# One streaming MoE layer on one core: the down weights of an expert loaded as one transfer of four chunks

## The reference

```
gu = xe @ w_gu[e] + b_gu[e]              # (rows, 1024) @ (1024, 2048)
g, u = gu[:, :D_FF], gu[:, D_FF:]
g = minimum(g, 7); u = clip(u, -7, 7)
h = (u + 1) * (g * sigmoid(1.702 * g))   # (rows, 1024), the inner features
y = h @ w_down[e] + b_down[e]            # (rows, 1024) @ (1024, 1024)
```

## Time and profile before

| | us |
|---|---|
| median of 3 runs | 1076.94 (1076.07 to 1077.82) |
| the profiled execution, its own time | 1075.5 |
| its span, first to last instruction | 1073.6 |
| PE (TensorE matmul) busy | 1029.4 (96%) |
| VectorE busy | 317.7 (30%) |
| ScalarE busy | 95.7 (9%) |
| DMA, mean over the span | 391 GB/s, 420.31 MB moved |

### The profile page before, as it was taken

One profiled execution on the slowest core, in us unless ns is written; L12 is line 12 of the kernel. 1 busy time (PEld: TensorE's weight loads), 2 busy tenths in 40 slices (PEclk: granted clock), 3 DMA queues, 4 the chain that ended last, 5 costly groups with the idle time before them and its releaser, 6 DMA issues.

```text
span 1073.6 us, 11705 instructions
## 1 busy us (share of the span) xinstructions
PE 1029.4 (96%) x5101; PEld 491.1 (46%) x5102; DVE 317.7 (30%) x491; ACT 95.7 (9%) x163; POOL 8.3 (1%) x20
## 2 busy tenths in 40 slices
PE   9999999999999999989898989989898989999997
PEld 7767454444444443435353534434353435334333
DVE  3533121332323232322313231323223132313243
ACT  2222130100000000000001010000000010100001
POOL 1100000000000000000000000000000000000000
PEclk9999999999999999999999999989999999999999
DMA  9950779999999999999999999999999999999996
GB/s 356 312 118 1 258 279 408 427 427 427 426 428 427 429 428 429 429 429 426 429 429 429 429 429 430 428 427 429 428 429 429 429 430 428 427 418 418 422 421 263
DMA packets 58543, 420.31 MB, mean 391 GB/s; under 512 B 23045, under 2 KB 23345, under 8 KB 29969
## 3 DMA queue, kind: packets, MB, share of 16 engines
q1 hardware_dynamic: 55840, 419.32, 94.6%
q0 software_dynamic: 352, 0.55, 0.2%
q10 hardware_dynamic: 2320, 0.03, 0.1%
HBM read 418.29 MB, written 1.58 MB: 391 GB/s over the span
## 4 chain that ended last, share of the span: by engine, by line
PE 68%; DMA 30%; issue 0%; SPq 0%; DVE 0%; ACT 0%; DVEq 0%
PE ps L854 35%; DMA ring<-in_w_gu_dram 28%; PE ps L787 7%; PE ps L870 6%; PE ps L709 5%; PE ps L896 3%; PE ps L727 3%; DMA ring<-in_w_down_dram 2%; PE ps L585 2%; PE ps L856 1%; PE ps L881 1%; PE ps L738 1%; PE ps L900 1%; PE ps L1024 1%; PE ps L611 1%; PE ps L677 0%
## 5 line engine op out<-in xcount | busy, mean ns | idle before, releaser
L854 PE MATMUL ps<-ring,xT 128*64 128x512 f32 x1008 | 457.3, 607 | 31.5 <-DMA ring<-in_w_gu_dram 31.3
L856 PE MATMUL ps<-ring,xT 128*64 128x512 f32 x1024 | 464.7, 607 | 0.0
L854 PEld LDWEIGHTS ps<-ring,xT 128*64 128x64 f32 x1008 | 135.6, 139 | 306.4 <-issue 301.9
L870 PE MATMUL ps<-ring,he 128*64 128x512 f32 x480 | 213.5, 594 | 3.4 <-DMA ring<-in_w_down_dram 2.5
L872 PE MATMUL ps<-ring,he 128*64 128x512 f32 x472 | 210.5, 596 | 0.0
L1613 DVE TENSOR_TENSOR x<-ps,x 128x512 f32<-128x512 f32 (+1 forms) x84 | 54.3, 683 | 297.8 <-PE ps L896 271.8
L856 PEld LDWEIGHTS ps<-ring,xT 128*64 128x64 f32 x1024 | 137.6, 139 | 0.0
L870 PEld LDWEIGHTS ps<-ring,he 128*64 128x64 f32 x480 | 63.1, 137 | 133.6 <-issue 133.6
L787 PEld LDWEIGHTS ps<-oh,hn 128*128 128x128 f32 x720 | 89.5, 196 | 8.3 <-issue 6.0
L787 PE MATMUL ps<-oh,hn 128*128 128x128 f32 x720 | 91.5, 282 | 0.0
L1256 ACT COPY gu_sb<-ps 128x1024 f32<-128x1024 f32 x16 | 16.2, 1012 | 607.4 <-PE ps L856 607.4
(11 more groups left out here) (220 smaller groups left out, 623.4 us busy)
## 6 DMA issues: line engine op xcount, KB each, us to landing
ring<-in_w_gu_dram SPq DMA_DIRECT2D x105, 2048.0 KB, 25.8
ring<-in_w_down_dram SPq DMA_DIRECT2D x53, 2048.0 KB, 27.0
ring<-in_w_gu_dram SPq DMA_DIRECT2D x44, 1024.0 KB, 19.6
ring<-in_w_down_dram SPq DMA_DIRECT2D x19, 1024.0 KB, 27.0
w_chc<-in_w_in_dram SPq DMA_DIRECT2D x1, 4096.0 KB, 20.7
w_qkv<-in_w_in_dram SPq DMA_DIRECT2D x4, 768.0 KB, 9.0
w_b<-in_w_in_dram SPq DMA_DIRECT2D x1, 2048.0 KB, 28.3
w_o<-in_w_out_dram SPq DMA_DIRECT2D x2, 1024.0 KB, 28.2
```

The source lines that it names most:

```text
L854: even = mm(gu_banks(j)[0:CAP, n, :], xT[j % 2][:, k, 0:CAP], first[n], start=(k == 0), stop=(k == KT - 1))
L856: odd = mm(gu_banks(j)[CAP:P, n, :], xT[j % 2][:, k, CAP:P], second[n], start=(k == 0), stop=(k == KT - 1))
L870: even = mm(out[0:CAP, half, :], hid[:, f, 0:CAP], first[2 * a + half], start=(f == 0), stop=(f == FT - 1))
```

## The change

An expert's four down chunks get one layout: partition p holds eight neighbouring features of w_down, 32 KB together (`dn_dram` loses its block index), and a load may take up to four chunks (`DN_RUN`). In `ORDER` all four down chunks of the even expert now come before the four of the odd one, where before they alternated by two. `features` takes every eighth column instead of every fourth, the biases come in two transfers of 32 bytes together instead of four of 16, and the values that TensorE waits for are worked out for each load (`per_pass`), since slots no longer all get the same number of loads. FINE, the tail loaded in the order of use, goes from 36 places to 40. The loads of w_gu stay as they are, in size and order.

```diff
-        dn_dram = w_down.rearrange("l e (m p a) n -> (l e) m p (a n)", a=2 * FPC, p=P)
+        GU_RUN, DN_RUN = 2, DNC
+        dn_dram = w_down.rearrange("l e (p a) n -> (l e) p (a n)", p=P)
...
-            for pair, chunks in ((j, range(GUC)), (j - 1, range(GUC, CH))):
+            for pair, chunks, run in ((j, range(GUC), GU_RUN), (j - 1, range(GUC, CH), DN_RUN)):
                 if 0 <= pair < PAIRS:
                     IN_USE += [(2 * pair + s, c) for c in chunks for s in range(2)]
-                    ORDER += [(2 * pair + s, c + a) for c in chunks[::2] for s in range(2) for a in range(2)]
+                    ORDER += [(2 * pair + s, c + a) for c in chunks[::run] for s in range(2) for a in range(run)]
...
-        EARLY, FINE = 3 * GUC, 4 * GUC + 4
+        EARLY, FINE = 3 * GUC, 5 * GUC
...
         while n < RINGED - 2:
-            e, c = ORDER[n]
-            two = (EARLY <= n < RINGED + 1 - FINE and c % 2 == 0 and ORDER[n + 1] == (e, c + 1)
-                   and slot_of(n) < RING - 1)
-            LOADS.append((n, 1 + two))
-            n += 1 + two
+            (e, c), many = ORDER[n], 1
+            room = min(RING - slot_of(n), RINGED - 2 - n, GU_RUN - c % GU_RUN if c < GUC else CH - c)
+            while n >= EARLY and many < room and ORDER[n + many] == (e, c + many):
+                many += 1
+            LOADS.append((n, many))
+            n += many
...
         def features(part, f):
-            m, a = f // (2 * FPC), f % (2 * FPC)
-            first = part * FF + m * 2 * FPC * P + a
-            return slice(first, first + 2 * FPC * (P - 1) + 1, 2 * FPC)
+            first = part * FF + f
+            return slice(first, first + FT * (P - 1) + 1, FT)
...
-                    for q in range(2 * FF // (4 * P)):
-                        sp.dma_start(b_guT[:, :, 4 * q:4 * q + 4],
-                                     b_gu[0].rearrange("e (q p a) -> q p e a", p=P, a=4)[q]).then_inc(bias_in, 16)
+                    for q in range(2):
+                        sp.dma_start(b_guT[:, :, FT * q:FT * (q + 1)],
+                                     b_gu[0].rearrange("e (q p a) -> q p e a", p=P, a=FT)[q]).then_inc(bias_in, 16)
...
-                pe.wait_ge(told, so_far(j, value, PER_LOOP // RING * 16))
+                pe.wait_ge(told, so_far(j, value, per_pass(e, c)))
...
+            def per_pass(e, c):
+
+                return LANDED[(e + 4, c)][1] - LANDED[(e, c)][1] if e + 4 < NE else 0
```

More of the change, by code:

```diff
@@ L309, in hybrid_layer_kernel @@
         ADDED_LATE = 2 * NT * (PAIRS - 2) - 2 * NT
-        gu_dram = w_gu.rearrange("l e (m p a) f -> (l e) m p (a f)", a=2, p=P)
-        dn_dram = w_down.rearrange("l e (m p a) n -> (l e) m p (a n)", a=2 * FPC, p=P)
+        GU_RUN, DN_RUN = 2, DNC
+        gu_dram = w_gu.rearrange("l e (m p a) f -> (l e) m p (a f)", a=GU_RUN, p=P)
+        dn_dram = w_down.rearrange("l e (p a) n -> (l e) p (a n)", p=P)
         IN_USE, ORDER = [], []
         for j in range(PAIRS + 1):
-            for pair, chunks in ((j, range(GUC)), (j - 1, range(GUC, CH))):
+            for pair, chunks, run in ((j, range(GUC), GU_RUN), (j - 1, range(GUC, CH), DN_RUN)):
                 if 0 <= pair < PAIRS:
                     IN_USE += [(2 * pair + s, c) for c in chunks for s in range(2)]
-                    ORDER += [(2 * pair + s, c + a) for c in chunks[::2] for s in range(2) for a in range(2)]
+                    ORDER += [(2 * pair + s, c + a) for c in chunks[::run] for s in range(2) for a in range(run)]
         ALL = len(IN_USE)
-        EARLY, FINE = 3 * GUC, 4 * GUC + 4
+        EARLY, FINE = 3 * GUC, 5 * GUC
         ORDER[:EARLY] = IN_USE[:EARLY]
@@ L327, in hybrid_layer_kernel @@
         EARLY_AT, LATE_AT, PIECES_AT = (1, CH - 1), (NE - 2, 0), (NE - 4, 0)
+        assert sorted(ORDER) == sorted(IN_USE)
         for at in (EARLY_AT, LATE_AT, PIECES_AT):
@@ L370, in features @@
         def features(part, f):
-            m, a = f // (2 * FPC), f % (2 * FPC)
-            first = part * FF + m * 2 * FPC * P + a
-            return slice(first, first + 2 * FPC * (P - 1) + 1, 2 * FPC)
+            first = part * FF + f
+            return slice(first, first + FT * (P - 1) + 1, FT)
         def tile_features(k):
-            first = k // 2 * 2 * P + k % 2
-            return slice(first, first + 2 * P - 1, 2)
+            first = k // GU_RUN * GU_RUN * P + k % GU_RUN
+            return slice(first, first + GU_RUN * (P - 1) + 1, GU_RUN)
         def most_rows(eng):
@@ L410, in rows_of @@
             def rows_of(e, c, many):
-                src = gu_dram[e, c // 2] if c < GUC else dn_dram[e, (c - GUC) // 2]
-                return src[:, c % 2 * FLAT:(c % 2 + many) * FLAT]
+                src, first = (gu_dram[e, c // GU_RUN], c % GU_RUN) if c < GUC else (dn_dram[e], c - GUC)
+                return src[:, first * FLAT:(first + many) * FLAT]
             def load(e, c, many, slot):
@@ L526, in _ @@
             pool.dma_start(w_rt[:, :, :], w_router.rearrange("l (k p) e -> p (l k) e", p=P)).then_inc(router_in, 16)
-            pool.dma_start(g2[:, :].rearrange("p (m a) -> p m a", a=2),
-                           norm2_g.rearrange("l (m p a) -> p (l m) a", a=2, p=P)).then_inc(router_in, 16)
+            pool.dma_start(g2[:, :].rearrange("p (m a) -> p m a", a=GU_RUN),
+                           norm2_g.rearrange("l (m p a) -> p (l m) a", a=GU_RUN, p=P)).then_inc(router_in, 16)
             pool.dma_start(b_rt[:, :], b_router.to_broadcast([P, NE])).then_inc(router_in, 16)
@@ L911, in chunks_of @@
                     [(2 * j - 2 + s, c) for s in range(2) for c in range(GUC, CH)]
+            def per_pass(e, c):
+                return LANDED[(e + 4, c)][1] - LANDED[(e, c)][1] if e + 4 < NE else 0
             for j in IN_LOOP[2:]:
                 for (e, c) in chunks_of(j):
-                    told, value = LANDED[(e - 4, c)]
+                    first = e - (j - IN_LOOP[0]) // 2 * 4
                     assert ORDER.index((e, c)) == ORDER.index((e - 4, c)) + PER_LOOP
-                    assert LANDED[(e, c)] == (told, value + PER_LOOP // RING * 16)
-            ARRIVALS = sorted({LANDED[at][1] for j in IN_LOOP[:2] for at in chunks_of(j)})
+                    assert LANDED[(e, c)][0] is LANDED[(first, c)][0]
+                    assert per_pass(e - 4, c) == per_pass(first, c) > 0
+            ARRIVALS = sorted({(LANDED[at][1], per_pass(*at)) for j in IN_LOOP[:2] for at in chunks_of(j)})
             GROWING = ([(value, 2) for value in range(1, 6)] + [(value, 2 * 2 * NT) for value in range(2, 2 * 2 * NT + 1, 2)]
-                       + [(value, PER_LOOP // RING * 16) for value in ARRIVALS])
+                       + ARRIVALS)
             growing = {}
@@ L1632, in _ @@
                 if j == 1:
-                    dve.wait_ge(bias_in, 4 * 16)
+                    dve.wait_ge(bias_in, 2 * 16)
                     gate_and_up(1, gu_banks(0), 0)
```

## The result

| kernel | median us | against before, 95% interval | its span |
|---|---|---|---|
| before | 1076.94 (5 runs) | | 1073.6 |
| with the change | 1081.60 (5 runs) | 1.0045 (1.003 to 1.0059) | 1078.7 |

The change makes the kernel 0.45% slower: 4.7 us. The forecast was +5.4 us, 1082.3.

A forecast was written before the change was run, and what follows sets the result against it. The prediction took DMA to bound the middle and a TensorE chain hanging on one landing the end. Wait +9.8, given back -4.0, clock +1.7 and rate -2.1 made +5.4 us: 1082.3 us, range 1078.3 to 1088.

The forecast's parts named there:

- The bound and the mechanism: DMA bounds the middle; the last 128 us are a TensorE chain hanging on one landing, so late waits decide.
- The new wait, +9.8: Pair 12's first down matmul must wait for all eight down chunks, beginning at 927.6 instead of 917.80: +9.8 us.
- The rate, -2.1: In the load stream, 26 four-chunk loads before pair 12's down each save a fixed 0.08 us: -2.1 us.
- The 2 us for each DMA: Skill's fixed cost per DMA: 24 loads fewer would give an estimated 48 us if uncovered; the queue was said to cover it.
- What is given back, -4.0: After pair 12's wait, later idle times of 0.29, 2.13, 1.32 and 0.3 us swallow part of the lateness: -4.0 us.
- The transposes, 0: Reading every eighth column in the transposes after pair 12's wait: taken as 0, bounded by 3.4 us either way.
- The clock, +1.7: After pair 12's longer wait TensorE runs a stretch at half clock that nothing absorbs: +1.7 us, ends 0 and 2.9.
- The sum: Whole kernel: 9.8 - 4.0 + 1.7 - 2.1 = +5.4 us, 1082.3 us, 0.5% slower; chance 0.72.
- rival a: Load stream runs dry, DMA engines idling 1 to 2 us in each of ten steps: 1092 to 1102 us; chance 0.09.
- Rival (b): Wider rows speed the load stream, pair 12's landing falls before 920: faster, about 1074 us; chance 0.05.
- (c): No difference: unseen slack in TensorE's end chain, or more rate gain, full clock and shorter wait: 1076 to 1079; chance 0.09.
- (d): The tail's single down chunks flow worse, partitions lying 32 KB apart with 8 KB read: +6 more, 1088 us; chance 0.05.

The follow-up runs named there:

- The run in two blocks: The change's order and four-chunk loads in the layout of the kernel before, each partition getting two rows of 16 KB: 1085.81 us, 1.0075 against before.
- the best kernel here: The changed kernel with TensorE's loop ending at pair 11 and the down chunks of pairs 11 and 12 loaded by two: 1075.71 us, 0.9989 against before.
- the kernel before with the shorter loop: The kernel before with TensorE's loop over pairs 2 to 11 and the last four pairs written out, nothing else: 1077.20 us, 1.0004 against before.

## Why the prediction was right

**The bound and the mechanism.** Right: the chain of TensorE work that hangs on pair 12's first down matmul set the end, and the waits moved to the first down of each pair from the third step with down work on. The rule "the last late landing counts" was tested by taking four-chunk loads from pair 12 (-6.5 us) and then from pair 11 (0.9 us more, at the edge of noise, but the waits came back where they should). As put, with no word on the pairs before, it was incomplete: had pair 12 been spared alone, I would have given too much back.

**The new wait, +9.8.** With the rate's share, -2.1, it was to be +7.7 us at that matmul; measured +8.65 and 9.4 (926.45 and 927.17 against 917.80). The graded delays of 0.4, 6.1 and 9.4 us for four, six and eight chunks needed, in executions of one group, confirm its cause. Of the waits that were to show it (3.5 to 5.5 us), eight of the eleven came so and three were shorter, 2.26 to 2.79; nine of the eleven were followed by a low clock.

**The rate, -2.1.** By itself right: 58.73 to 58.58 us a step is 0.15, two loads of 0.08. The run in two blocks shows that it is the packet that costs. What the forecast lacks is about 1 us at the start of the stream: a load of the changed kernel issued at 232.9 landed 14.4 us later, at 247.3, where before it was 246.3. In the nine profiles with the new order this landing lies between 246.7 and 249.2 us, in the four with the old one between 246.2 and 247.3. The ranges overlap, and the cause stays open.

The 2 us for each DMA that the prediction cites are given by that section of the Trainium skill ("DMA: Bandwidth & Descriptors", "Anatomy of one DMA") for DMAs issued by GpSimd. These are issued by SyncE, and the trace doesn't show such a cost: two loads fewer gain 0.15 us a step.

**What is given back, -4.0.** The term was too small: by the starts of the same matmuls in both kernels, 4.6 us were given back. It read only the idle times that the timeline lists, and one wait of pair 12 is not listed. In the kernel before, the second halves landed at 927.5, and the third down call began 0.70 us after the matmul ahead of it instead of the 0.43 between neighbours:

```profile
926.88 0.59 PE L870 MATMUL ps<-ring,he 128*64 128x512 f32 x1
...
927.58 0.61 PE L870 MATMUL ps<-ring,he 128*64 128x512 f32 x1
```

These 0.27 us went too. The down part of pair 12 up to the next `gate_up` took 934.97 - 917.80 = 17.17 us and takes 942.67 - 926.45 = 16.22: 0.95 less, of which 0.27 is this wait, 0.15 the transposes and 0.53 what the listed 0.29 was worth. In the same way the listed 2.13 was worth 2.24, and 1.32 was worth 1.57. Each of these three waits cost 0.1 to 0.25 us more than its idle time. The 0.3 us of the weight loads gave nothing: from the first matmul of the last pair to the end it is 25.4 us in both.

**The transposes, 0.** Off by 0.15 us a pair in the good direction. Their weight loads answer to the earlier trace rows with 192 ns instead of 210: every eighth column is read faster than every fourth, and 16 transposes take 1.96 us instead of 2.13. The run with the layout alone has 191 ns, the one in two blocks, with the old layout, 210.

```profile
L885 PEld LDWEIGHTS ps<-ident,gu_sb 128*128 128x128 f32 x256 | 29.6, 192 | 13.5 <-issue 13.5
...
286.09 1.96 PE ps L885 x16
```

**The clock, +1.7.** In size right (1.5 and 2.7 us in the two executions of the change), in place only by half: that the first execution paid it at all is luck. In the profiled execution no low clock followed the 2.41 us wait; it came at 962.3, in the gather of pair 14:

```profile
961.80:966.30 4.50, 4.50 (x25) 4.42 (x24) 0.69 (x1) 0.00 (x0) 0.00 (x0) 0.62 1.00 417
976.79:979.80 3.01, 3.01 (x25) 2.90 (x24) 0.68 (x1) 0.00 (x0) 0.00 (x0) 1.00 1.01 419
```

The first row is that gather, the second the next one, which is the same work at full clock: 4.5 against 3.0 us. What lowered the clock there is not known.

**The sum** for the profiled execution: +8.65, less 4.6 at the waits and 0.45 of transposes, plus 1.5 of clock = 5.1 us. The forecast had +7.7, less 4.0, plus 1.7 = 5.4. That the two lie 0.3 us apart is in part luck: the landing was 0.95 us later than forecast, and the waits, the transposes and the clock together gave 1.25 us more back.

**The stream running dry** (rival a) did not happen. The load issued after m = 2 at 242.3, the thinnest point, landed 10.0 us later, at 252.3, 5.0 us behind the one before it: its own transfer time.

```profile
L419 SPq DMA_DIRECT2D ring<-in_w_gu_dram x1: 328/328/328, 242.3 to 242.3; - x1
...
DMA to landing us min/median/max: 10.0/10.0/10.0
```

Later the stream is full as well (430 GB/s from 400 to 860 us, above). Rival (b) falls with the steps of 58.58 us, (c) with the measured 1081.60, and (d) with the layout alone at 1075.99.

## What to carry to other kernels

When transfers are merged, write down for every consumer which byte it waits for before and after: a merged load and a merged order delay the first use by the bytes put in front of it (here four chunks of 1 MiB: 9.8 us by their transfer time, 8.7 and 9.4 measured), while the gain is 0.08 us a load. In a kernel with slack in its middle such a wait costs nothing there and its full price near the end, so merge in the middle and go back to small, alternating loads some steps before the end: lateness divided by what the consumer catches up in a step (9.8 / 5.5, two pairs) says how many. Even so, the best kernel here is only 0.1% faster than the one before. A fine tail isn't free either: single 8 KB rows flow 1.6% slower (421 against 428 GB/s), and lengthening it starved the end of the kernel before.

## What was not expected of the hardware

The granted clock fell to its lower level (1.2 of 2.4 GHz) in four of the twelve profiles of the changed kernel and the experiments (near 962, 966, 967 and 978 us) while TensorE had been busy without a listed idle time for at least 30 us. Each time it covered a gather in pair 14's step (the first one, at 978 the second), which took 4.6 us from start to end instead of 3.1, and stayed low for 3.4 us. The Trainium skill ("TensorE: Matmul & The Clock Gate", Part 1) ties the half rate to an engine that was idle; these four do not agree.

Nor did the length of a wait alone decide. In the kernel before with the shorter loop, a wait of 3.67 us was followed by full clock (the matmul took its 0.61 us) and one of 2.09 us by a low clock (the next matmul took 0.91):

```profile
703.49 0.61 PE L854 MATMUL ps<-ring,xT 128*64 128x512 f32 x1 [3.67 <-DMA ring<-in_w_gu_dram]
...
946.95 0.61 PE L854 MATMUL ps<-ring,xT 128*64 128x512 f32 x1 [2.09 <-DMA ring<-in_w_gu_dram]
...
947.40 0.91 PE L854 MATMUL ps<-ring,xT 128*64 128x512 f32 x1
```

Reading transposed operands at a stride of eight floats was faster than at four (192 against 210 ns a weight load).
